# S5 mixer and gate placed between the blocks of the input projection, and prompt and decode cross attention interleaved, with cache loads issued earlier

## Chip, cores and metric

The kernel is written in Bass and runs on one core of one Trainium2 chip. The metric is the device time of one execution in microseconds (us). The kernel before takes 1489.02 us, the median of three runs (1488.8 to 1489.31).

## The reference

One layer of a hybrid decoder. A prompt of 512 tokens and 8 decode requests of 8 tokens each go through the same weights; the kernel treats them as T = 576 columns. All tensors are float32, D = 1024.

```
h = x + 1/2 * SwiGLU(rms_norm(x))                      # w_ffn1, F = 2816
u = rms_norm(h);  q,k,v,zg,r,us5 = split(u @ w_in)     # 256,256,512,16,512,512 columns
GLA (4 heads, dk 64, dv 128): log_a = log_sigmoid(zg @ w_gate + b)/16,
    S_t = diag(a_t) S_{t-1} + k_t^T v_t,  o_t = q_t S_t;  o = rms_norm(o) * silu(r)
S5 (32 groups x 16 channels, 64 complex states): x_t = A x_{t-1} + B u_t,
    y = Re(C x) + D u;  z = gelu(y);  out = z * sigmoid(z @ w_glu + b)
h = h + concat(GLA, S5) @ w_out
mk, mv = split(rms_norm(mem_prompt) @ w_ckv)           # 256 memory tokens, 4 heads of 256
h = h + CrossAttn(rms_norm(h) @ w_cq, keys, values) @ w_co
    # the prompt attends to mk, mv; each decode request to its own cached keys and values
h = h + 1/2 * SwiGLU(rms_norm(h));  y = rms_norm(h)    # w_ffn2
```

The new GLA and S5 states and mk, mv are outputs too. The cached keys and values of a request are 256 x 1024 numbers each, 1 MB; there are 8 of each.

## The kernel before

**Projections.** Every weight matrix is cut into blocks of 128 output columns, in the order of the list `groups` (first feed-forward, W_IN, W_IN+1, W_OUT mixed with KV, W_Q, W_O, second feed-forward). SP loads block n into one of four buffers `raw`; it waits until block n-4 has been converted. ACT's `conv(n)` copies it to a high half `wh` (L1102), DVE's `conv(n)` forms the low half `wl` (L1365), both two blocks ahead of PE. PE's `dense` does three products (high-high, high-low, low-high) in 8 k steps and two column halves of 288: 48 matmuls of L604 a block, into PSUM banks 0 to 3. DVE evicts a block when PE has finished it, and `ps_free` and `w_lo` let the block after next go. Most PE instructions that are not turns (transposes) go through one helper, L604.

**Input projection.** W_IN gives q, k, v, W_IN+1 gives r and the S5 input u; both write `PR`. Between the two, ACT issues eight DMAs that spread Kt into TT (L1180). Behind W_IN+1 PE does the 16-column gate rank (h, wzg).

**S5 and gate stage.** It starts when all projection blocks are done. PE turns u (L741), turns it again into u2 (L749), does the gate's products, the input products (Win x u2, stationary from Hs), the products with TT, then those with XS and CA, turns of states (L790 to L792), of v (L799), of the gelu result z (L811), and the GLU products. Between these DVE and ACT work: copies out of PSUM (L1525, L1529), ACT's crosswise copies (L1202), rotation by tables (L1540 to L1543), one scan over all chunks (L1546), rotation back (L1549 to L1553), the gate's log and its scans, gelu (L1216), copies of v (L1618) and z (L1621), then sigmoid (L1232), product (L1627), high copy (L1235), low half (L1637). POOL builds keep5 (L571) and scales q (L574). Level operations for GLA (L1579 to L1590) are put between the sigmoid steps. GLA's seven levels follow: PE's small products, and `take` on DVE (L1598).

**Cross attention.** When W_Q is done, the prompt's four row blocks of 128 go one after another: scores (8 products), maxima on DVE (L1749), exponentials on ACT (L1307), division on DVE (L1754), eight turns on PE (L1000), copy (L1761); the next block's scores are issued ahead. Then eight value products of 512 columns, twice each. Only then the eight decode requests: 16 turns of the keys (L1016) in two halves, copied by ACT (L1325) and DVE (L1787), with scores of 32 stationary columns a head; then decode softmax and values. SP loads the caches (L377) into four buffers `KB`, keys 0 and 1 when W_Q is done, keys 2 and 3 when the last prompt scores are, the rest as buffers come free.

Of the kernel before, what the change touches and what calls it, by code (L numbers as in the profile page):

```python
# [6 lines left out]
F32 = mybir.dt.float32  # L7
# [6 lines left out]
P = 128  # L14
# [37 lines left out]
def hymba_kernel(nc, A, O, consts):  # L52

    with ExitStack() as ctx:
# [90 lines left out]
        kem = view(AR, 4 * T, NB, 2, DK)  # L145
# [32 lines left out]
        u2 = view(Xs, 0, G, C5)  # L178
        SF = Xs[:, 2304:6400]
        UT = SF[0:C5, :].rearrange("p (g s q) -> p g s q", g=G, s=L5)  # L180
        zin = view(SF, 0, G, C5P)
        zz = view(SF, 2048, G, C5P)
        Y2 = SF[0:C5, :].rearrange("p (t j) -> p t j", t=L5)
        SG = Xs[:, 6400:8704]
        XS = view(SG, 0, G, C5)
        keep5 = view(SG, 0, G, C5P)
        wglu = view(Xs, 8704, 4, P)
        zin_tmp = SF[:, 2048:4096]
        zT = view(SG, 0, 4, T)
        sig = view(Xs, 0, T)  # L190
        sog = view(Xs, 576, T)
        s1o = view(MM, 8448, 3, P)

        Snew = view(AR, 12 * T, 2, NB, DV)
# [3 lines left out]
        mh = view(ARr, 8 * T, KD, M)  # L198
# [6 lines left out]
        KB = [view(Xs, 4096, 2, D), view(Xs, 6144, 2, D), view(MM, 0, 2, D), view(MM, 2048, 2, D)]  # L205
        KBT = view(MM, 8192, KD, M)
        pp = view(Xs, 0, H, M)
        att = view(Xs, 1024, 16)
        os = view(Xs, 1040, 2, M)

        qz = view(Xs, 2048, KD, NB, 4 * BT)
        PTz = view(MM, 4096, 2, H, NB, 4 * BT)
# [12 lines left out]
        def add(kind, src, nblk, K, row0, cols, **kw):  # L225
            n0 = sum(g["n"] for g in groups)
            groups.append(dict(kind=kind, src=src, n=nblk, K=K, row0=row0, cols=cols, n0=n0, **kw))
# [10 lines left out]
        add("proj", A["w_in"], 8, KD, 0, (0, P, 2 * P), f0=0, first=True)  # L238
        add("proj", A["w_in"], 8, KD, 0, (D + RANK, D + RANK + P, 2 * P), f0=8)
# [54 lines left out]
        def _(e):  # L294
# [31 lines left out]
            def load(n):  # L326

                g, i = blocks[n]
                K, (c0, c1, step) = g["K"], g["cols"]
                col = (i // 2) * step + (c0, c1)[i % 2]  # L330
# [18 lines left out]
            load(3)  # L349
            for n in range(4, groups[W_O]["n0"] + 4):  # L350
                load(n)
                if n % 2:
                    parameters((n - 3) // 2)
                if n == groups[W_OUT]["n0"] + 5:
                    e.wait_ge(S("zt_mm"), L5)
# [11 lines left out]
            for n in range(2 * NB):  # L367
                if n < 2:
# [231 lines left out]
        def _(e):  # L600
# [171 lines left out]
            for r in range(8):  # L772
                if r == 4:
                    e.wait_ge(S("d_ok"), 5)
# [1084 lines left out]
```

## Time and profile before

| | |
|---|---|
| median of three runs | 1489.02 us |
| profiled execution, its own time | 1489.69 us |
| its span in the profile | 1487.9 us |
| mean granted clock of PE | 0.956 |
| busy: PE, weight loads, DVE, ACT, POOL | 93%, 89%, 46%, 28%, 19% |
| bytes moved | 130.2 MB, 88 GB/s |

The time of an execution is a little longer than the span between its first and last recorded instruction. A granted clock of 1.0 is 2.4 GHz, 0.5 is 1.2 GHz; a value between is the mean of a stretch with both. A matrix product in float32 leaves two records a matmul, a turn one. Positions in the trace are us from the start of the span.

### The profile page before, as it was taken

What the parts mean: (1) busy time and instruction counts of PE and PEld (TensorE: products, weight loads), DVE (VectorE), ACT (ScalarE), POOL (GpSimd) and SP (SyncE); (2) the same over time, 40 slices, a digit from 0 to 9 for tenths busy, and PEclk for the clock granted to TensorE, in tenths of its full rate; (3) what the DMA queues carried; (4) which work ended last, traced back from release to release, by engine and by line L of the source; (5) the groups of instructions that cost most, each with busy time, mean ns of one, the idle gap of its engine ahead of it and who ended that gap; (6) DMA issues with size and microseconds to landing.
All of it is one profiled execution on the core that took longest, in us unless ns stands there. A gap on an engine that the chain in (4) does not pass through costs nothing.

```text
span 1487.9 us, 24142 instructions
## 1 busy us (share of the span) xinstructions
PE 1383.2 (93%) x10626; PEld 1324.0 (89%) x10626; DVE 689.2 (46%) x817; ACT 422.6 (28%) x550; POOL 287.1 (19%) x372
## 2 busy tenths in 40 slices
PE   5999999999999989866799996989999999999997
PEld 4999999999998988856789894559999999999997
DVE  5444258635444324786664534324443334433442
ACT  4322122212234111452443212213422122212233
POOL 3001799887022002000011000003100000000012
PEclk9999999999999999776899997989999999999998
DMA  6433222322222352010144342462223222232221
GB/s 167 98 90 85 86 72 85 86 86 72 75 82 57 85 102 74 1 33 6 57 130 140 97 148 81 142 226 86 73 84 86 86 86 78 79 86 85 78 65 65
DMA packets 227049, 130.20 MB, mean 88 GB/s; under 512 B 22192, under 2 KB 221296, under 8 KB 226928
## 3 DMA queue, kind: packets, MB, share of 16 engines
q1 hardware_dynamic: 219552, 123.22, 28.6%
q10 hardware_dynamic: 7392, 5.43, 1.7%
q8 instruction: 84, 1.38, 0.4%
q14 instruction: 21, 0.17, 0.0%
HBM read 121.67 MB, written 5.78 MB: 86 GB/s over the span
## 4 chain that ended last, share of the span: by engine, by line
PE 84%; DVE 10%; ACT 2%; issue 2%; DMA 1%; ACTq 1%; POOLq 0%; POOL 0%; DVEq 0%
PE PS L604 80%; DVE wl L1365 1%; PE PS L1016 1%; ACTq L1180 1%; DMA AR<-in_cache_mem_v 1%; DVE gua L1442 1%; ACT Xs L1307 1%; DVE AR L1598 0%; PE PS L1000 0%; DVE Xs L1754 0%; DMA gua<-in_g_mem 0%; DVE AR L1761 0%; DVE Xs L1749 0%; DVE Xs L1621 0%; DVE Xs L1546 0%
## 5 line engine op out<-in xcount | busy, mean ns | idle before, releaser
L1102 ACT ACTIVATE wh<-raw 128x1024 fp32r<-128x1024 f32 (+1 forms) x192 | 200.6, 1045 | 794.8 <-PE PS L604 794.8
L604 PE MATMUL PS<-xh,wh 128*128 128x288 f32 x1792 | 388.1, 298 | 16.4 <-DVE wl L1365 11.0
L604 PE MATMUL PS<-xh,wl 128*128 128x288 f32 x1792 | 385.7, 297 | 0.0
L604 PE MATMUL PS<-xl,wh 128*128 128x288 f32 x1792 | 385.3, 297 | 0.0
L604 PEld LDWEIGHTS PS<-xh,wh 128*128 128x128 f32 x1792 | 290.3, 190 | 18.8 <-DVE wl L1365 12.2
L604 PEld LDWEIGHTS PS<-xh,wl 128*128 128x128 f32 x1792 | 290.5, 190 | 0.0
L604 PEld LDWEIGHTS PS<-xl,wh 128*128 128x128 f32 x1792 | 290.4, 190 | 0.0
L1365 DVE TENSOR_TENSOR wl<-raw,wh 128x1024 fp32r<-128x1024 f32 (+1 forms) x192 | 259.1, 1349 | 56.6 <-ACT wh L1102 54.9
L407 POOL TENSOR_TENSOR acc<-acc,sq 128x576 f32<-128x576 f32 x40 | 68.0, 1700 | 772.8 <-issue 537.4
L604 PE MATMUL PS<-yh,wh 128*128 128x288 f32 x960 | 207.6, 298 | 1.0 <-DVE yl L1802 1.0
L604 PE MATMUL PS<-yl,wh 128*128 128x288 f32 x960 | 206.3, 297 | 0.0
L604 PE MATMUL PS<-yh,wl 128*128 128x288 f32 x960 | 206.0, 296 | 0.0
L604 PEld LDWEIGHTS PS<-yh,wh 128*128 128x128 f32 x960 | 155.3, 190 | 1.6 <-DVE yl L1802 1.4
L604 PEld LDWEIGHTS PS<-yl,wh 128*128 128x128 f32 x960 | 155.4, 189 | 0.0
L604 PEld LDWEIGHTS PS<-yh,wl 128*128 128x128 f32 x960 | 155.3, 189 | 0.0
L1417 DVE SCALAR_TENSOR_TENSOR h<-PS,h 128x576 f32<-128x576 f32 x56 | 42.4, 758 | 191.0 <-PE PS L604 191.0
L416 POOL TENSOR_TENSOR AR<-AR 128x32 f32<-128x32 f32 (+6 forms) x168 | 112.1, 667 | 13.6 <-POOL AR L529 0.4
L1439 DVE TENSOR_TENSOR gua<-PS,R 128x576 f32<-128x576 f32 x44 | 33.4, 758 | 156.2 <-PE PS L604 156.1
L1435 DVE TENSOR_TENSOR gua<-PS,R 128x576 f32<-128x576 f32 x44 | 33.3, 756 | 108.3 <-PE PS L604 108.3
L604 PE MATMUL PS<-AR 64*64 64x64 f32 (+5 forms) x640 | 63.8, 345 | 7.1 <-DVE AR L1598 3.7
L604 PEld LDWEIGHTS PS<-AR 64*64 64x64 f32 (+3 forms) x640 | 44.8, 175 | 24.9 <-issue 10.1
L1507 DVE TENSOR_TENSOR AR<-PS,R 128x576 f32<-128x576 f32 x24 | 18.2, 757 | 88.8 <-PE PS L604 75.4
(297 smaller groups left out, 1108.8 us busy)
## 6 DMA issues: line engine op xcount, KB each, us to landing
raw<-in_w_ffn_gu SPq DMA_DIRECT2D x88, 512.0 KB, 3.8
raw<-in_w_ffn_down SPq DMA_DIRECT2D x32, 512.0 KB, 4.0
raw<-in_w_in SPq DMA_DIRECT2D x16, 512.0 KB, 4.0
raw<-in_w_ckv SPq DMA_DIRECT2D x16, 512.0 KB, 3.9
raw<-in_w_ffn_down SPq DMA_DIRECT2D x16, 384.0 KB, 3.4
raw<-in_w_out SPq DMA_DIRECT2D x8, 512.0 KB, 4.4
raw<-in_w_cq SPq DMA_DIRECT2D x8, 512.0 KB, 4.2
raw<-in_w_co SPq DMA_DIRECT2D x8, 512.0 KB, 4.2
```

What stands on the lines that cost most here:

```text
L407: e.tensor_tensor(acc[:, 0:T], acc[:, 0:T], sq[:, k % 2, :], ALU.add).then_inc(acc_ready, 1)
L416: own(TTT(o, a, b, ALU.mult))
L604: return e.matmul(out, lhsT, rhs, start=start, stop=stop, **kw)
L1016: last = e.transpose(bank(0, P, at=f * M + j * P), KB[b % 4][:, j, f * P:(f + 1) * P], ident)
L1102: e.activation(wh[:, n % 2, 0:K * P], raw[:, n % 4, 0:K * P], ACT.Copy).then_inc(w_hi, 1)
L1180: e.dma_start(TT[P5 * s:P5 * s + P5, :, P5 * s:P], Kt[:, :, 0:P - P5 * s]).then_inc(S("tt_in"), 16)
L1307: e.activation(pp[0:w, hd, :], bank(4 * (1 - r % 2), H, M, rows=w)[:, hd, :], ACT.Exp, bias=att[0:w, 4 + hd:5 + hd], scale=CD ** -0.5, acc ...
L1365: TTT(wl[:, n % 2, 0:K * P], raw[:, n % 4, 0:K * P], wh[:, n % 2, 0:K * P].bitcast(F32), ALU.subtract).then_inc(w_lo, 1)
L1417: STT(two(hk), halves(2 * par), 0.5 if g["half"] else 1.0, two(hk), ALU.mult, ALU.add).then_inc(ps_free, 1)
L1435: TTT(two(gs[:]), halves(0), two(R[:]), ALU.mult).then_inc(g_scaled, 1)
L1439: TTT(two(us[:]), halves(2), two(R[:]), ALU.mult).then_inc(ps_free, 1)
L1507: TTT(two(chunk(PR, f)), halves(2 * par), two(R[:]), ALU.mult).then_inc(ps_free, 1)
```

## The change

It has two parts.

- The input projection is one run of 16 blocks in the order u, q, k, v, r. PE's S5 and gate work is cut into pieces, and `beside(b, i)` issues one behind k step i of block b: gate rank in block 4, turns of u in 5, of u2 in 6, input products in 7 and 8, gate products in 10, TT and XS products in 11 and 12, turns of z in 13, of v in 14, GLU in 15. DVE's and ACT's `beside(b)` do their share behind their work for block b. The small products use banks 4 to 7 only, and the S5 buffers have moved to Hs and AR. TT's DMAs are issued by SP, two behind each of four weight loads; copies of v are ACT's now, and every second copy of z.
- Cross attention is written as one hand-made order on PE, DVE and ACT: turns of a request's keys, decode scores of the request before, and every third step the scores, turns or values of a prompt row. Keys are copied by head instead of by half. Decode scores run with f outside and heads inside. Keys 0 to 3 are loaded during the W_Q blocks into Hs, 4 and 5 when W_Q is done; the values each have a place of their own as soon as it is free. Waits for `gla_out` come before W_Q on DVE, `kv_out` on ACT moves to W_O.

The core of the diff:

```diff
-        add("proj", A["w_in"], 8, KD, 0, (0, P, 2 * P), f0=0, first=True)
-        add("proj", A["w_in"], 8, KD, 0, (D + RANK, D + RANK + P, 2 * P), f0=8)
+        add("proj", A["w_in"], 8, KD, 0, [D + RANK + (4 + i) * P for i in range(4)] + [i * P for i in range(4)])
+        add("proj", A["w_in"], 8, KD, 0, [(4 + i) * P for i in range(4)] + [D + RANK + i * P for i in range(4)])
...
+                if n > groups[W_Q]["n0"] and (n - groups[W_Q]["n0"]) % 2 and n < groups[W_O]["n0"]:
+                    e.wait_ge(mm_done, M0 + MIX.rindex("W") + 3)
+                    load_cache((n - groups[W_Q]["n0"]) // 2)
...
+                s0 = 2 * (n - groups[W_IN]["n0"] - 5)
+                if 0 <= s0 < L5:
+                    e.wait_ge(S("tt_zero"), 1)
+                    e.wait_ge(S("ktd_ok"), 1)
+                    for s in (s0, s0 + 1):
+                        e.dma_start(TT[P5 * s:P5 * s + P5, :, P5 * s:P], Kt[:, :, 0:P - P5 * s]).then_inc(S("tt_in"), 16)
...
+            def beside(b, i):
+
+                if b == 4:
+                    gate_rank(i)
+                elif b == 5:
+                    turn_u(i)
+                elif b == 6 and i < 5:
+                    turn_u2(i)
+                elif b == 7 and i % 3 == 0:
+                    input_products(i // 3)
+                elif b == 8 and i in (1, 4):
+                    input_products(3 + i // 4)
+                elif b == 10 and i in (0, 2):
+                    gate_products(i // 2)
+                elif b in (11, 12) and i % 2:
+                    s5_outputs(4 * (b - 11) + i // 2)
+                elif b == 13:
+                    turn_z(i)
+                elif b == 14 and 2 <= i < 7:
+                    turn_v(i - 2)
+                elif b == 15 and i % 2:
+                    glu(i // 2)
+
+            n0 = groups[W_IN]["n0"]
+            for b in range(16):
+                dense(n0 + b, b % 2, KD, xh, xl, ready=(x_lo, 8) if b == 0 else None,
+                      inside=(lambda: rms(1), KD - 3) if b == 0 else None, each=lambda i: beside(b, i))
+            e.wait_ge(ps_free, n0 + 18)
+            e.wait_ge(S("sig_ok"), 4)
...
+            def decode_scores(b):
+                if b == 0:
+                    e.wait_ge(S("qz_ok"), 4)
+                e.wait_ge(S("kbt_a"), 2 * b + 2)
+                e.wait_ge(S("kbt_v"), 2 * b + 2)
+                for f in range(2):
+                    for hd in range(H):
+                        last = mm(PS[32 * hd:32 * hd + 32, 7, (b // 4) * M:(b // 4 + 1) * M], qz[:, 2 * hd + f, b, :],
+                                  KBT[b % 2][hd][:, f, :], start=(b % 4 == 0 and f == 0), stop=(b % 4 == 3 and f == 1),
+                                  skip_group_check=True)
...
+            turn_keys(0)
+            prompt_scores(0)
+            turn_keys(1)
+            decode_scores(0)
+            turn_keys(2)
+            decode_scores(1)
+            prompt_scores(1)
+            prompt_turn(0)
+            turn_keys(3)
+            decode_scores(2)
...
+            decode_scores(7)
+            prompt_turn(3)
+            decode_values(0)
+            for f in range(4):
+                prompt_values(f)
+            decode_turn(1)
+            for f in range(4, 6):
+                prompt_values(f)
+            decode_values(1)
+            decode_out_turn(0)
+            for f in range(6, 8):
+                prompt_values(f)
+            decode_out_turn(1)
...
-            for s in range(L5):
-                e.dma_start(TT[P5 * s:P5 * s + P5, :, P5 * s:P], Kt[:, :, 0:P - P5 * s]).then_inc(S("tt_in"), 16)
...
+            def beside(b):
...
+                elif b == 9:
+                    rotate_back(0)
+                    e.wait_ge(S("z_mm"), 1)
+                    for i in range(2):
+                        mark(TSC(two(zb[:, i, :]), halves(4 + 2 * i), bgate[:, i:i + 1], None, ALU.add), "z_sb")
```

## Rows read from the trace of the kernel before

**Rows 1.** The page, busy time and share of the span by engine.
```profile
PE 1383.2 (93%) x10626; PEld 1324.0 (89%) x10626; DVE 689.2 (46%) x817; ACT 422.6 (28%) x550; POOL 287.1 (19%) x372
```
**Rows 2.** Stretches: length, busy PE, PEld, DVE, ACT, POOL, then clock, DMA, GB/s.
```profile
592.20:667.55 75.35, 57.78 (x420) 51.40 (x419) 60.35 (x82) 34.49 (x56) 4.36 (x7) 0.77 0.07 19
602.00:620.00 18.00, 18.00 (x89) 18.00 (x90) 12.68 (x23) 8.66 (x14) 0.00 (x0) 0.53 0.00 1
620.00:624.00 4.00, 4.00 (x39) 4.00 (x38) 3.96 (x2) 1.69 (x2) 0.49 (x1) 1.00 0.00 0
...
888.20:995.00 106.80, 83.29 (x521) 50.49 (x521) 39.85 (x70) 23.57 (x55) 5.47 (x7) 0.86 0.48 168
```
**Rows 3.** Timeline of PE, S5 stage: start, length, line, shapes, count, idle before.
```profile
592.22 3.72 PE L741 MATMUL PS<-cst,AR 128*72 128x128 f32 x32
596.81 2.20 PE L749 MATMUL PS<-cst,Xs 72*128 72x72 f32 x32 [0.87 <-DVE Xs L1525]
...
601.91 13.62 PE L604 MATMUL PS<-Xs,Hs 128*128 128x72 f32 x64
...
628.63 8.85 PE L604 MATMUL PS<-AR,Xs 128*72 128x128 f32 x64 [4.19 <-DVE Xs L1553]
...
652.89 6.50 PE L604 MATMUL PS<-Xs 128*128 128x288 f32 x16 [0.83 <-DVE Xs L1621]
```
**Rows 4.** Timelines of ACT's queue and of PE between W_IN and W_IN+1.
```profile
526.71 13.47 ACTq L1180 DMA_DIRECT2D Hs<-AR  x8
...
544.28 0.85 PE L604 MATMUL PS<-xh,wh 128*128 128x288 f32 x2 [4.95 <-DVE wl L1365]
```
**Rows 5.** Chain that ended last, one prompt row's softmax: start, length, what.
```profile
908.34 1.24 DVE Xs L1749
...
909.80 1.94 ACT Xs L1307 x8
```
**Rows 6.** The same chain, decode keys and scores, then decode values.
```profile
946.75 1.02 PE PS L1016 x8
947.77 0.99 PE PS L604 x8
...
976.57 3.75 PE PS L604 x64
...
980.34 10.28 DMA AR<-in_cache_mem_v
```
**Rows 7.** The same chain, turns of mk and mv inside a W_Q block.
```profile
846.90 0.44 PE PS L971 x4
847.34 0.80 PE PS L604 x6
```
**Rows 8.** Timeline of DVE in the S5 stage.
```profile
618.96 4.42 DVE L1546 TENSOR_TENSOR_SCAN Xs<-Xs 128x2048 f32<-128x2048 f32 x1
...
655.99 0.76 DVE L1627 TENSOR_TENSOR Xs<-Xs 128x576 f32<-128x576 f32 x1 [1.76 <-ACT Xs L1232]
...
667.55 1.33 DVE L1598 COPY_PREDICATED AR<-cst,PS 128x512 f32<-128x512 int32 x2
```
**Rows 9.** Groups of 584 to 668, and line L1365 (duration ns min/median/max, 200 to 300).
```profile
L1365 DVE TENSOR_TENSOR wl<-raw,wh 128x1024 fp32r<-128x1024 f32 x1 | 4.1, 4061 | 0.4 <-ACT wh L1102 0.4
L574 POOL TENSOR_SCALAR AR<-AR 128x1152 f32<-128x1152 f32 x1 | 4.0, 3985 | 0.1
...
L1365 DVE TENSOR_TENSOR wl<-raw,wh x16: 1225/2182/3425, 200.6 to 297.2; 128x1024 fp32r<-128x1024 f32 x16
```
**Rows 10.** Timeline of PE in the cross attention.
```profile
898.22 1.10 PE L1000 MATMUL PS<-cst,Xs 128*128 128x128 f32 x8 [2.00 <-DVEq L1755]
...
906.88 3.62 PE L604 MATMUL PS<-AR 128*128 128x256 f32 x16
...
925.58 16.26 PE L604 MATMUL PS<-AR 128*128 128x512 f32 x32 [1.32 <-DVE AR L1761]
```
**Rows 11.** Stretch after that first gap, columns as in rows 2.
```profile
900.00:902.00 2.00, 2.00 (x6) 1.58 (x5) 1.93 (x3) 0.00 (x0) 0.00 (x0) 0.50 0.04 8
```

More of the change, by code:

```diff
@@ L1199, in _, with swap @@
                     e.wait_ge(S("d_ok"), r - 1)
-                d, dw = bank(4 + r % 4, n, C5), view(zin_tmp, 512 + 512 * (r % 2), n, C5P)
+                d, dw = bank(4 + r % 4, n, C5), dw_buf[r % 2][:, 0:n * C5P].rearrange("p (g c) -> p g c", g=n)
                 for a in (0, 64):
                     e.activation(dw[64 - a:128 - a], d[a:a + 64, :, 0:C5P], ACT.Copy).then_inc(S("dw_ok"), 1)
-            e.wait_ge(S("z_sb"), 2)
-            mark(e.activation(zt, zb, ACT.Abs), "act_own")
-            mark(e.activation(zt, zt, ACT.Exp, scale=-1.0), "act_own")
-            mark(e.activation(zt, zt, ACT.Ln, bias=one[:]), "ln_ok")
-            for half in range(2):
+            def swap(half):
                 gg = slice(16 * half, 16 * half + 16)
@@ L1210, in _, with gelu @@
                 e.activation(zin[0:64, gg, :], zz[64:128, gg, :], ACT.Copy).then_inc(S("swap_a"), 1)
-            e.wait_ge(S("s1_ok"), 1)
-            e.wait_ge(S("swap_a"), 2)
-            for r in range(8):
+            def gelu(r):
                 e.wait_ge(S("y_mm"), r + 1)
@@ L1237, in _ @@
+            n0 = groups[W_IN]["n0"]
+            for b in range(16):
+                if b == 0:
+                    rms(1)
+                conv(n0 + b + 2)
+                beside(b)
+            e.wait_ge(S("y_mm"), 8)
+            e.activation(EB, zb, ACT.Exp, scale=1.0 / TAU).then_inc(S("eb_ok"), 1)
             for j in range(NT):
@@ L1310, in softmax_decode @@
             def softmax_decode(c):
[L1311 to L1317 removed]
+                e.wait_ge(S("mx_ok"), ROWS["decode"][c])
+                e.activation(ppd[:, c, :], bank(7, M, at=c * M), ACT.Exp, bias=attd[:, 4 + c:5 + c],
+                             scale=CD ** -0.5, accum_out=attd[:, 8 + c:9 + c]).then_inc(S("exp_ok"), 1)
@@ L1319, in _ @@
                 e.activation(yh[:, f, 0:TP], bank(4 + f % 2, TP), ACT.Copy).then_inc(S("pv_hi"), 1)
[L1320 to L1327 removed]
+            e.wait_ge(gla_out, 64)
@@ L1328, in _, with decode_high @@
+            keep_keys(0)
+            softmax(0)
+            keep_keys(1)
+            keep_keys(2)
+            softmax(1)
+            keep_keys(3)
+            keep_keys(4)
+            softmax(2)
+            softmax_decode(0)
+            keep_keys(5)
+            keep_keys(6)
+            softmax(3)
+            keep_keys(7)
             softmax_decode(1)
-            for c in range(2):
+            for f in range(6):
+                values_high(f)
+            def decode_high(c):
                 e.wait_ge(S("ost_mm"), c + 1)
```

715 lines of the change are left out of this document (409 added, 306 removed).

## Prediction

> **What bounds the kernel now.** The page's busy times come first: PE works in 93% of the span, so only three things can be won: time in which PE stands idle, time in which it runs at half its clock, and PE work itself [rows 1]. Next the stretches: two stages are neither projections nor feed-forward, and PE is poorly used in both. From the end of the input projection's rank-16 products (592.2) to the first predicated copy of the GLA levels (667.55) lie 75.4 us, with PE busy for 57.8 and a mean granted clock of 0.77. The cross attention, from the last query block to the first w_co matmul (888.2 to 995.0), takes 106.8 us, PE busy 83.3, clock 0.86 [rows 2]. Then the timelines say why. In the first stage PE, DVE and ACT hand the S5 work to one another. PE was busy all through 602 to 620, but at 0.53 of its clock; at the full clock, 620 to 624, it issues 39 records in 4 us [rows 2, 3]. Before that stage there is one more stop, at 544.28: PE had waited 4.95 us for a low weight half, because ACT was issuing eight DMAs (TT from Kt) for 13.47 us ahead of its conversions [rows 4]. In the second stage the softmax of each of the four prompt rows is a round trip PE, DVE, ACT, DVE, PE [rows 5], and near its end PE waits for the value caches: one DMA stands in the chain with 10.28 us [rows 6].
>
> **S5 and gate beside the projection.** The same PE instructions are issued, but between the k steps of sixteen dense blocks. That this costs no more than the instructions themselves is seen where the kernel does it already: four transposes take 0.44 us, the six matmuls behind them 0.80, and no gap is left [rows 7]. 6 in 0.80 makes 6.4 us for a block of 48; this is in both kernels and drops out, as do the rank-16 products.
> What is inserted, at the full clock: 32 turns of u 3.7; 32 turns for u2 2.2; 32 turns of z in the same 72x72 shape 2.2; 20 turns of v at u's 0.117 each 2.3 [rows 3]. Input products: 64 records took 13.62 at half clock, so 6.8. TT and XS: 128 records at 4.00/39 are 13.1 [rows 2, 3]. Gate and GLU: 16 records took 6.50 at half clock, so 24 at 0.2 are 4.9 [rows 3]. Three state turns 0.4. Sum 36 us. The upper bound is the pace of before, some 55 us, which they would cost only if PE fell to half clock; between dense matmuls it has no reason to.
> DVE and ACT have to keep up. DVE was busy 60 us in the old stage [rows 2]; with sixteen evictions (0.76, the price of 576 columns) and low halves (1.23) that is 92 us in about 16 x 6.4 + 8 + 36 = 146 [rows 8, 9]. So DVE is no bound over the whole, but single blocks can be late. I followed block by block (E8 is the end of dense block 8): the rotation of chunk 4 ends at E8 + 4.1, the scan takes 4.42 [rows 8], so DVE comes 2.2 us late to block 9's eviction. A low half has about 4 us of slack, so dense work does not stop there. But rotate_back(0) and the gate's bias come behind, and S5 output 0 in block 11 waits for z_sb: 1 to 4 us. ACT puts Abs, Exp, Ln ahead of the next conversion, rotate_back(1) comes behind that, and gelu behind s1_ok: up to 1 us in block 12. The GLU of block 15 waits for sigmoids that stand behind five ACT operations and a table load: 1.3. First turns in blocks 6, 7 and 13: 0.1 to 0.5 each. That is about 5 together.
> POOL adds to it. It now scales q (3.98 us) and builds keep5 beside the u2 copies and the first rotations. Where these two ran before, DVE's low half took 4.06 us against 1.23 at best [rows 9]. So I add 2 us of stall for the chain pushed later, with 0 and 5 as bounds. The Trainium skill, "SBUF — State Buffer", Who interferes with whom, says that VectorE and GpSimd share a port pair which one of them holds for a whole instruction while the other is blocked. The rows agree, 4.06 against 1.23; by that rule every DVE operation with two SBUF inputs that meets one of POOL's waits out its rest, by these rows up to 2.8 us a meeting, and two meetings in a row would make the 2 us a 5.
> **The tail.** After block 15 DVE finishes the sigmoid chain (sigmoid, product, copy and subtraction at some 0.75 each, about one and three quarters rounds late: 5.1), then evicts (0.8), converts (1.25), forms KE over 1152 columns (1.4), and does four pairs of level operations at 0.7 each that before were hidden in the wait for sigmoids (5.7): 14.3 us to the first predicated copy [rows 8]. This part stays exposed, and GLA after it is untouched.
> Before: 75.4, plus 4.95 for the stop at 539 and 1.5 for a restart at half clock [rows 2, 4]. After: 36 + 7 + 14.3 = 57.3. **Gain 24.5 us**, bounds 5 (all that is inserted at half clock) and 33 (no stall, tail 2 shorter).
> The TT DMAs go to SP's queue, two behind each of four weight loads: 13.47 us of issue in all [rows 4], over four blocks of 6.4. Behind them stand only weight loads issued about three blocks ahead of use, so nothing is late; if that cover were gone, the stop of 5 us would come back. UT shares memory with Kt, so DVE and ACT wait for tt_in in block 5; by then the last has been issued for about a block. The eight small DMAs of wglu stay on ACT, ahead of need.
>
> **Cross attention.** PE work after, at full clock: four prompt scores at 3.62 are 14.5; four turns of probabilities at 1.02 are 4.1; eight key turns of 16 transposes at 2 x 1.02 are 16.3; the prompt's values 13.8: 16 products of 512 columns, twice the 0.45 of 256 would be 14.5, and 16.26 is what they took with half clock in front, from which I take off its first 2.5 [rows 6, 10]. Decode scores: before, four products on two column groups took 0.99, so 15.8 in all; the new order runs f outside and heads inside, so four column groups follow one another as in the decode values, where 32 products took 3.75, or 0.94 for eight. I take 8 x 0.94 = 7.5 as that row has the same pattern; the other bound is 15.8 [rows 6]. Decode values 7.5, small turns 2.3. Sum 66 us.
> Idle: in each of four rounds DVE takes the maxima (1.24 and 0.18), ACT the exponentials (1.94) [rows 5], and ACT's key copies stand behind them, so the third or fourth quarter of a key turn waits about 2.5 us: 9 with the last DVE steps. Clock: the gap of 2.0 us before 898.22 was enough to leave 900 to 902 at 0.50 [rows 10, 11]; by that row the 2.5 us gaps can each cost 1.7 more; I add 3 of 7. End of the stage: 66 + 9 + 3 = 78 against 106.8 and 1.5 for the slow restart of w_co. **Gain 30.3 us**, bounds 18 and 38.
> The caches: K0 to K3 go out in the query blocks, behind weight loads with slack. The other 12 have 78 us; before, they moved in 46 (945 to 991), so the 10.28 us leave the chain [rows 6]. V7 waits on the third decode values product (about 54 us in) and is used at 65: 11 us against a landing of 10.3 at worst; 0 to 3. The w_co weights from the fifth on stand behind V7 on SP, but are used 20 us later. The earlier waits for gla_out find DMAs issued 80 us before, and POOL's memset of PTz ends about a microsecond ahead of need: nothing.
>
> **Sum.** 1489.69 (the profiled execution; span 1487.9) - 24.5 - 30.3 = 1434.9; the median of the runs is 0.67 lower, so 1434.2.
>
> **Rivals.** (a) The round trips cost less: 2 us of stalls in S5, none for the clock, 2 fewer in attention: 1434 - 5 - 3 - 2 = 1424. For: each wait rests on an order that I guessed. (b) Decode scores stay at 0.99 per four (+8.3) and each attention gap halves the clock (+4): 1446. For: the rows show both; against: the row of the values [rows 6, 11]. The Trainium skill, "TensorE: Matmul & The Clock Gate", HAM oscillation, tells that repeated waits bring the slow clock back every time; the window at 900 agrees. (c) The S5 chain is a block late somewhere, through POOL or ACT's order: 6.4 and some 7 more idle, 1448. (d) Slower than before: PE works in order, so an S5 piece that waits for DVE now stops dense matmuls too. With eleven blocks that carry pieces this is slower than before from 5.2 us of waiting per block (57 over 11). The largest wait for DVE in front of these pieces was 4.19 us, once [rows 3], and DVE has 92 us of work in 146: unlikely; 1500. (e) The change does not do what it says: the pieces wait until the projection is over, or cache loads hold up weights: 1480 to 1489.
>
> **How the numbers follow.** Forecast 1434 (1427 to 1442) 0.50; (a) 0.17; (b) 0.13; (c) 0.14; (e) 0.03, of which 0.02 within 0.2% (3 us, about what a measurement can tell); (d) 0.03. The range 1416 to 1456 leaves out (d), (e) and the outer parts of (a) and (c), some 0.15. Faster 0.95, same 0.02, slower 0.03.
>
> **What would show it.** No gap in front of the second half of the input projection; its blocks 5 to 15 at clock 1.0, 36 us longer together than 6.4 each; a gap of 1 to 4 us in block 11; about 14 us from the last GLU product to the first predicated copy; an attention of 78 us, with eight decode score products in 0.94 and no cache DMA in the chain. A block longer than its sum by over 5 us, half clock in the projection, or scores at 2 us for eight would make it wrong.

## The result and the profile after

| kernel | median, us | lowest to highest | ratio to before, 95% interval |
|---|---|---|---|
| before | 1488.91 | 1486.32 to 1489.31 | 1 |
| after | 1438.53 | 1437.9 to 1438.6 | 0.9664 [0.9648, 0.9681] |

The change takes 50.4 us off, 3.4%; 1434.2 was forecast. The profiled execution of after has a span of 1436.7 us, 51.2 less than the 1487.9 of before, and a mean granted clock of 0.973 (0.956 before).

The page of after, first the busy line that answers to [rows 1], then the chain that ended last by engine:

```profile
PE 1352.5 (94%) x10626; PEld 1303.9 (91%) x10626; DVE 682.3 (47%) x816; ACT 428.1 (30%) x567; POOL 287.3 (20%) x372
...
PE 86%; DVE 9%; ACT 3%; issue 2%; DMA 0%; ACTq 0%; POOLq 0%; POOL 0%; DVEq 0%
```

The number of PE records is the same, 10626. PE is busy 31 us less because it does the same work at a higher clock (and with more products side by side), and stands idle 20 us less. The stretches of after that answer to [rows 2], same columns (length, busy time of PE, PEld, DVE, ACT, POOL, clock, DMA share, GB/s): first the whole input projection with the S5 pieces in it up to the first predicated copy, a piece inside it, the tail behind the last GLU product, then the attention from the last query block to the first w_co product, and two pieces inside it.

```profile
472.92:643.03 170.11, 158.40 (x1231) 145.24 (x1231) 89.92 (x110) 62.99 (x88) 11.58 (x9) 0.97 0.28 64
602.00:620.00 18.00, 18.00 (x151) 17.45 (x150) 10.47 (x16) 9.01 (x12) 0.26 (x1) 1.00 0.21 59
628.47:643.03 14.56, 5.32 (x88) 4.02 (x88) 12.26 (x16) 9.28 (x14) 0.00 (x0) 0.59 0.42 108
865.25:945.08 79.83, 67.44 (x522) 45.51 (x520) 41.28 (x78) 23.93 (x63) 4.31 (x6) 0.96 0.49 172
860.00:900.00 40.00, 33.10 (x261) 27.54 (x259) 20.76 (x34) 13.08 (x39) 1.99 (x4) 1.00 0.51 184
900.00:920.00 20.00, 16.33 (x127) 11.98 (x127) 11.39 (x24) 5.02 (x14) 2.32 (x2) 0.83 0.57 211
```

The same stretch of before, from the first product of the input projection to the first predicated copy, is this one. It holds nearly the same records (1223 against 1231) in 23.4 us more:

```profile
474.05:667.55 193.50, 170.98 (x1223) 158.90 (x1223) 98.40 (x120) 53.98 (x75) 11.98 (x9) 0.90 0.25 57
```

The attention went from 106.80 us [rows 2] to 79.83. So the 51.2 us are: 1.1 before the input projection starts (474.05 to 472.92), 23.4 in it and the S5 stage, 27.0 in the attention, 1.3 behind it, less 1.6 between the first predicated copy and the end of W_Q (220.6 us before, 222.2 after). That last 1.6 is no effect of the change that these traces can show: the same kernel took 218.6 us there in another execution, and kernels whose edits lie elsewhere 221.2 to 222.1.

Where PE now stands idle. In the projection and S5 stage, its timeline shows one stop of any size among the dense blocks, the first S5 output in block 11, which waits for the gate's bias; the pieces behind it come every 3.34 us, two k steps of 0.80 and 1.74 of their own. The idle time is in brackets with what ended it.

```profile
574.14 1.06 PE L633 MATMUL PS<-Hs,AR 128*72 128x128 f32 x8 [1.97 <-DVE gua L1723]
...
577.50 1.04 PE L633 MATMUL PS<-Hs,AR 128*72 128x128 f32 x8
...
624.68 1.24 PE L633 MATMUL PS<-AR,Hs 128*128 128x288 f32 x4 [0.37 <-ACT sq L1359]
627.34 1.13 PE L633 MATMUL PS<-AR,Hs 128*128 128x288 f32 x4
635.31 2.42 PE L633 MATMUL PS<-AR 64*64 64x64 f32 x72 [6.84 <-DVE AR L1807]
```

The stop of 4.95 us [rows 4] is gone. In the attention PE waits for ACT's copies of turned keys (L1456) and for the decode softmax:

```profile
875.19 0.66 PE L1095 MATMUL PS<-cst,Hs 128*128 128x128 f32 x4 [2.67 <-ACT Xs L1456]
...
887.46 0.66 PE L1095 MATMUL PS<-cst,Hs 128*128 128x128 f32 x4 [1.79 <-ACT Xs L1456]
...
900.26 0.66 PE L1095 MATMUL PS<-cst,Xs 128*128 128x128 f32 x4 [2.32 <-ACT Xs L1456]
...
913.93 0.41 PE L1114 MATMUL PS<-cst,Xs 128*128 128x128 f32 x2 [3.00 <-DVE AR L1947]
...
945.08 0.54 PE L633 MATMUL PS<-yh,wh 128*128 128x288 f32 x2 [1.72 <-DVE yl L1985]
```

### The profile page after: what moved, and what is told of

Its sections match the earlier page's. It is cut to its first block, busy times and chain, and to the rows that moved or that the text cites. A ratio compares the mean times of both kernels' runs of the same rounds, so it can differ in the third digit from the quotient of the medians.

```text
span 1436.7 us, 24185 instructions
## 1 busy us (share of the span) xinstructions
PE 1352.5 (94%) x10626; PEld 1303.9 (91%) x10626; DVE 682.3 (47%) x816; ACT 428.1 (30%) x567; POOL 287.3 (20%) x372
## 3 DMA queue, kind: packets, MB, share of 16 engines
q1 hardware_dynamic: 223280, 124.40, 30.3%
## 4 chain that ended last, share of the span: by engine, by line
PE 86%; DVE 9%; ACT 3%; issue 2%; DMA 0%; ACTq 0%; POOLq 0%; POOL 0%; DVEq 0%
PE PS L633 83%; DVE wl L1524 1%; PE PS L1095 1%; DVE gua L1601 1%; DVE AR L1791 0%; ACT wh L1209 0%; DMA gua<-in_g_mem 0%; ACT Xs L1442 0%; DVE Xs L1935 0%; PE PS L724 0%; DVE Hs L1718 0%; DVE Xs L1830 0%; DVE xl L1641 0%; DVE xl L1555 0%; DVE h L1645 0%
## 5 line engine op out<-in xcount | busy, mean ns | idle before, releaser
L633 PE MATMUL PS<-AR 64*64 64x64 f32 (+6 forms) x720 | 73.3, 339 | 13.8 <-DVE AR L1791 6.8
L633 PEld LDWEIGHTS PS<-AR 64*64 64x64 f32 (+4 forms) x720 | 52.7, 178 | 28.0 <-issue 13.4
L633 PE MATMUL PS<-ARr,wh 128*128 128x256 f32 x256 | 46.1, 282 | 0.8 <-DVE wl L1524 0.8
```

What stands on the lines that cost most here:

```text
L633: return e.matmul(out, lhsT, rhs, start=start, stop=stop, **kw)
```

## The experiments

Theory: the gain is PE's time, won in two independent stages; what is left lies in the tail behind the GLU and in the order in which ACT copies keys. Rivals: the stages depend on each other; the low price of the decode scores is a matter of their order; the early loads bring nothing; the slack of the S5 chain is large, or small. Eleven further kernels were run, and the kernel after once more. The kernel before ran beside each group; its median was between 1488.6 and 1490.2. The second time, after itself had a median of 1437.39 us with single executions from 1433.57 to 1441.0. By medians alone, then, only five kernels lie clear of after: the two single parts, the early outputs, and the new copy order alone and in the pair. For the others the cause is read from the waits and lengths in their traces.

### Each part alone

The S5 part with the attention of before, and the attention part with the S5 stage of before. In words, since the edits are the two halves of the diff; the one line added, in the first, keeps a wait where the new placement needs it:

```diff
+            e.wait_ge(gla_out, 64)      # DVE, now ahead of its W_Q group
```

> The S5 part of the change with the attention of the kernel before. My theory: the two parts don't touch each other, so this kernel keeps the gain read between the start of the input projection and the first predicated copy (193.50 to 170.20 us, 23.3), and loses about 1.4 us of it again in the W_Q stage: 1489 - 22 to 24 = 1465 to 1467 us. Its attention stage, from the last W_Q product to the first projection of the cross stage, is again about 107 us. Rival: the stages are coupled by the clock, and the gap of 14.7 us between the last gate product and the first predicated copy costs more in this kernel than in the whole change; then the time is 1470 or more.

Measured: 1463.85 us, ratio 0.9828 [0.9814, 0.9843], so 25.3 us gained, a little more than the 22 to 24 expected.

> The attention part of the change with the S5 stage of the kernel before. My theory: its gain is its own, 106.8 to about 80 us for the stage and so 1489 - 26 to 28 = 1461 to 1463 us; the two gains add up to the 50.4 of the whole. Rival: the early cache loads are hidden only because the S5 stage of the whole change left the DMA queues earlier, or they take from the weight transfers of W_Q; then less than 24 us are gained here and the sum of the two single kernels falls short of the whole by more than 2 us.

Measured: 1463.3 us, 0.9820 [0.9805, 0.9835], so 25.8 gained. The two make 51.1; the whole change gains 50.4. The stages don't depend on each other, and the early cache loads work without the new S5 stage. The attention part came out a little under its range of 26 to 28. In the attention of the first kernel PE still waits for the value caches, as in [rows 6], here at each of four groups of products, the longest time 2.40 us:

```profile
961.28 1.96 PE L612 MATMUL PS<-Xs,AR 128*32 128x256 f32 x16 [2.40 <-DMA Xs<-in_cache_mem_v]
```

### The order of the decode scores

```diff
-                for f in range(2):
-                    for hd in range(H):
+                for hd in range(H):
+                    for f in range(2):
```

> The changed kernel with one edit: the decode score products run over the halves of the contraction inside and the heads outside, as in the kernel before, so that two products that follow each other go to the same column group. My theory: the eight products of a batch took 0.94 to 1.07 us in the changed kernel because the four heads' products overlap, and in the kernel before a batch of four took 0.99 (eight records in 1.98 with both halves); this edit brings the second figure back for 8 batches: +0.9 each, +7 to 8 us, 1445 to 1447. Rival one: the overlap is between any products of different column groups however they are ordered, and the order costs half: +3 to 4, 1442. Rival two: the order does nothing, because the stage is held by the copies of the turned keys: within 1 us of 1438.5.

Measured: 1439.07 us, 0.9657 [0.9641, 0.9673]: nothing, as in rival two, but not for its reason. PE's timeline, first of after, then of this kernel; each x2 line is one product of two records, and the last line of each is the turn behind the eight.

```profile
888.05 0.41 PE L633 MATMUL PS<-Hs,AR 128*32 128x256 f32 x2
...
888.29 0.39 PE L633 MATMUL PS<-Hs,AR 128*32 128x256 f32 x2
...
889.05 2.06 PE L1095 MATMUL PS<-cst,Xs 128*128 128x128 f32 x16
```

```profile
888.86 0.42 PE L633 MATMUL PS<-Hs,AR 128*32 128x256 f32 x2
...
889.10 0.39 PE L633 MATMUL PS<-Hs,AR 128*32 128x256 f32 x2
...
889.88 2.07 PE L1095 MATMUL PS<-cst,Xs 128*128 128x128 f32 x16
```

Eight products take 1.00 us from the first to the turn in the one and 1.02 in the other. The prediction's reason, that heads inside lets column groups follow one another, falls. The size, 0.94, was right. What remains as a difference from before is how many column groups are at work between two instructions that take all columns: four here, two before. The next run tests that.

```diff
-            decode_scores(b)            # b = 0, 2, 4
-            turn_keys(b + 2)
+            decode_scores(b, (0, 1))
+            turn_keys(b + 2, (0, 1))
+            decode_scores(b, (2, 3))
+            turn_keys(b + 2, (2, 3))
```

> The changed kernel with the decode score products of batches 0, 2 and 4 parted: heads 0 and 1, then half of the key turns of batch b+2, then heads 2 and 3 and the other half. The order of the eight products did nothing (they took 1.07 us in either order), and in the kernel before four products of two heads, between key turns on all columns, took 0.99. My theory: what sets their time is how many column groups are at work between two products that take all columns: the records of one group follow each other (0.4 us each product), those of four groups overlap. Each half then takes 0.95 to 1.05 us and each parted batch 0.9 to 1.0 us more: +2.7 to +3 us in all, 1441 to 1441.5. Rival: the price belongs to the waits on the copies in the kernel before, not to the column groups: each half takes about 0.5 and the time stays within 0.5 us.

Measured: 1442.12 us, 0.9671 [0.965, 0.9693], some 3.6 us over after. PE's timeline:

```profile
889.26 0.66 PE L1095 MATMUL PS<-cst,Hs 128*128 128x128 f32 x4 [1.79 <-ACT Xs L1460]
889.85 1.06 PE L633 MATMUL PS<-Hs,AR 128*32 128x256 f32 x8
890.84 1.10 PE L1095 MATMUL PS<-cst,Xs 128*128 128x128 f32 x8
891.86 1.06 PE L633 MATMUL PS<-AR 128*32 128x256 f32 x8
892.85 1.42 PE L1095 MATMUL PS<-cst,Xs 128*128 128x128 f32 x8
894.21 1.07 PE L633 MATMUL PS<-Xs,AR 128*32 128x256 f32 x16
```

Each half takes 0.99 (889.85 to 890.84, 891.86 to 892.85): the price of before for four products, 0.99 [rows 6]. The unparted batch behind them (894.21, x16) takes 1.00 again. The parted batch costs 0.98 more, and its second eight turns 0.34 more than the first (1.36 from start to next start against 1.02), which the theory didn't have: 1.3 a batch. The same 0.34 stands at all three parted batches; its cause is open. By medians 3.6 us were measured for 2.7 to 3 expected. The theory holds for the scores: four products on two column groups cost what eight on four do, in either order. That it isn't a fixed price of each entry is seen in [rows 6]: there 64 records on four groups, 16 a group, took 3.75, or 0.23 for each record of a group; here four a group take 1.00, or 0.25. An estimate from these rows: with all eight batches in halves, as before, the scores would cost 8 us more.

The Trainium skill, "TensorEngine Tiling (Array Packing)", Key Properties, states that tiles operate independently and can execute in parallel. The rows agree and add that this held here whether the next product in order went to the same group or to another.

### The small DMAs on ACT

```diff
-                    for s in (s0, s0 + 1):            # SP, beside four weight loads
-                        e.dma_start(TT[...], Kt[...]).then_inc(S("tt_in"), 16)
+                if b == 1:                            # ACT, behind block 1
+                    for s in range(L5):
+                        e.dma_start(TT[...], Kt[...]).then_inc(S("tt_in"), 16)
```

> The changed kernel with the transfers that build the mixer's block matrix issued from ScalarE's stream, behind its second block, and not from SyncE's beside the weights. My theory of the 4.95 us wait on the second weight half in the kernel before: ScalarE's share of these issues had delayed what the block waits for. If so, ScalarE comes late with its copies by the time of the issues (8 of about 0.6 to 1.3 us, 5 to 8 us in all), TensorE waits for a copy once, and 3 to 6 us of the gain go: 1441 to 1445. Rival: ScalarE has that slack in the early blocks of the projection, and nothing changes: 1438 to 1439.5.

Measured: 1444.04 us, 0.9695 [0.9677, 0.9713]: 5.5 over after, the upper end. ACT's queue and, below it, PE:

```profile
486.35 14.09 ACTq L1307 DMA_DIRECT2D Hs<-AR  x8
...
502.91 0.55 PE L627 MATMUL PS<-xh,wh 128*128 128x288 f32 x2 [3.94 <-DVE wl L1523]
```

The eight issues take 14.09 us, as the 13.47 of [rows 4], and not the 5 to 8 that the expectation wrote down against its own row. The stop in front of a block is back, 3.94 us. On SP in after the four pairs take 1.33, 1.26, 2.78 and 2.46 us, 7.8 in all and not the 13.47 that the prediction carried over, and PE has no wait there.

### Late cache loads

```diff
-                if n > groups[W_Q]["n0"] and (n - groups[W_Q]["n0"]) % 2 and n < groups[W_O]["n0"]:
-                    e.wait_ge(mm_done, M0 + MIX.rindex("W") + 3)
-                    load_cache((n - groups[W_Q]["n0"]) // 2)
...
-            for n in range(4, 2 * NB):
+            for n in range(2 * NB):
```

> The changed kernel with all cache transfers issued behind the last W_Q block, so none is there when the attention starts. In the changed kernel a transfer lands 7.2 us (median) after its issue, and the key turns of the first batch start at once. My theory: the first key turn comes some 5 to 7 us late, because a first transfer needs that long; behind it the 16 transfers keep ahead of TensorE (each about 3.7 us of a queue share, against 9 us of TensorE a batch), so the loss is that first wait plus a clock that starts low: +5 to +9 us, 1443.5 to 1447.5. Rival one: the transfers in a bunch share the DMA engines and land later one by one, so that each batch waits: +15 or more, as in the kernel before. Rival two: TensorE's scores of the prompt stand ahead of the keys in its order only from the second place; the wait is longer than any cover: nothing is hidden, +7 to +9 with the full latency. An unchanged time would say that the early loads bring nothing.

Measured: 1443.44 us, 0.9687 [0.9665, 0.9708], 4.9 over after. PE's timeline where the attention starts, and the stretch of the whole attention in this kernel:

```profile
871.39 3.68 PE L1092 MATMUL PS<-cst,Hs 128*128 128x128 f32 x16 [5.07 <-DMA Hs<-in_cache_mem_k]
...
866.17:953.10 86.93, 70.78 (x522) 47.72 (x521) 41.05 (x78) 24.15 (x63) 4.34 (x6) 0.90 0.56 206
```

One wait of 5.07 us, then 16 turns at 3.68 in place of 2.06 because the clock is halved behind it, and no further wait for a cache. The attention is 7.1 us longer than in after, which is the first wait and the clock (0.90 for 0.96). Rival one, every batch waiting, is out; theory and rival two gave nearly the same time (the measured one is just under both), and what tells them apart is the wait, within the theory's 5 to 7. The whole profiled execution is 8.0 us longer than after's. Of that 1.6 lie in the S5 stage, where nothing was edited: PE's wait in block 11 is the same, 1.96, but here the clock was lower behind it (0.91 over 560 to 580, 1.00 in after).

### How much slack the S5 chain has

```diff
+                elif b == 10 and i >= 4:
+                    s5_outputs(i - 4)
-                elif b in (11, 12) and i % 2:
-                    s5_outputs(4 * (b - 11) + i // 2)
+                elif b == 11 and i % 2:
+                    s5_outputs(4 + i // 2)
```

> The changed kernel with the eight output pieces of the state mixer put half a block to a block earlier on TensorE: the first four in the second half of the projection's block 10, the other four in block 11, none in block 12. It measures how much slack the mixer's chain has: in the changed kernel the first of these pieces waits 2.0 us for VectorE's copy of the gate input at 572.4. My theory (the mechanism of my slower case): TensorE takes its instructions in order, reaches the first piece at about 568, and stands until about 572 with all of the block's products behind it; VectorE's eviction doesn't come earlier for it. The wait is 4 to 6 us in place of 2, and the later pieces wait for ScalarE's gate steps of the block before: +2 to +5 us, 1440.5 to 1443.5. Rival: VectorE is ready by then because its own order depends on TensorE's block 9 only, and nothing changes: 1438 to 1439.

Measured: 1451.0 us, 0.9739 [0.9724, 0.9754]: 12.5 over after, far outside the expected 2 to 5. PE's first stop, DVE's line behind it, PE's second stop, and two stretches:

```profile
573.55 1.95 PE L633 MATMUL PS<-Hs,AR 128*72 128x128 f32 x8 [5.96 <-DVE gua L1725]
...
584.31 0.76 DVE L1809 TENSOR_TENSOR AR<-PS,R 128x576 f32<-128x576 f32 x1 [10.87 <-PE PS L633]
...
592.18 1.98 PE L633 MATMUL PS<-Hs,AR 128*72 128x128 f32 x8 [4.65 <-ACT Hs L1306]
...
570.00:590.00 20.00, 13.99 (x94) 13.77 (x94) 8.55 (x10) 7.21 (x6) 0.00 (x0) 0.82 0.12 36
590.00:600.00 10.00, 7.82 (x49) 7.82 (x50) 1.35 (x2) 2.28 (x8) 1.09 (x2) 0.67 0.01 2
```

The first wait is as expected, 5.96 us, 4.0 more than after's. But a second of 4.65 follows, for ACT's gelu (L1306), and the first one feeds it. PE stood inside block 10, so that block ended late; DVE had to wait 10.87 us for it before its eviction (584.31). Behind the eviction and the low half stands the second half of the rotation back, which ends at 591.4; gelu starts at 591.48 when it is there, and PE's fifth output piece waits for gelu. PE waits for DVE, which waits for PE: the expectation had counted only the first half of that circle. And behind each wait the clock is halved for a while: 13.99 x 0.18 + 7.82 x 0.33 = 5.1 us. Waits of 8.6 more and 5.1 for the clock make 13.7; the stage is 183.73 us long against 170.11. So the chain does not have the slack of half a block to a block that this edit takes, and the mechanism of rival (d) is real: this one placement costs a quarter of the whole change's gain.

### GpSimd beside VectorE

```diff
+            for _ in range(3):
+                own(TTT(keep5, ..., ALU.mult))
             mark(TTT(keep5, ..., ALU.mult), "keep_ok")
```

> The changed kernel with GpSimd's product that builds the keep mask (3.63 us at 533.59) done four times, so that GpSimd works some 11 us longer beside VectorE's eviction, low half and first two rotations (535.3 to 545). In the changed kernel its one meeting with VectorE's low half stretched that from 1.23 to 1.89 us and TensorE did not notice. My theory: each VectorE operation with two SBUF inputs that meets a GpSimd operation waits for it to end; operations that read PSUM on one side don't. Low half and the rotation's second and third operations (0.62 each, four of them up to 545) are stretched, two to four meetings of 1 to 3 us; VectorE is 5 to 8 us late in block 7, the low half of the block after next has only some 4 us of slack, so TensorE stops for 1 to 4 us, and the clock may halve behind it: +1 to +5 us, 1439 to 1443. Rival: TensorE's slack swallows it all (as it did the one meeting), within 1 us of 1438. Second rival: both engines share and GpSimd's operations are the ones stretched; then VectorE's durations stay 0.62.

Measured: 1441.3 us, 0.9671 [0.9649, 0.9694], 2.8 over after. POOL's timeline (three of the four products in one line), then DVE's beside it, then PE's stop in block 11:

```profile
533.62 12.15 POOL L601 TENSOR_TENSOR AR<-AR,cst 128x2048 f32<-128x2048 f32 x3 [1.74 <-DVE AR L1709]
545.85 3.88 POOL L603 TENSOR_TENSOR AR<-AR,cst 128x2048 f32<-128x2048 f32 x1
...
538.81 0.62 DVE L1681 TENSOR_TENSOR Hs<-PS,AR 128x448 f32<-128x448 f32 x1 [0.48 <-ACT Hs L1297]
539.47 2.83 DVE L1682 TENSOR_TENSOR Hs<-Hs,AR 128x448 f32<-128x448 f32 x1
542.33 3.93 DVE L1683 TENSOR_TENSOR Hs<-Hs 128x448 f32<-128x448 f32 x1
...
576.08 1.06 PE L636 MATMUL PS<-Hs,AR 128*72 128x128 f32 x8 [3.88 <-DVE gua L1726]
576.98 1.72 PE L636 MATMUL PS<-AR 128*72 128x128 f32 x8
```

DVE's operations with both inputs in SBUF (L1682, L1683) took 2.83, 3.93 and (at 547.25) 2.98 us in place of 0.62; the ones with PSUM on one side (L1681) kept their 0.62 in the same time. These three cost DVE 7.9 us. PE noticed none of it before block 11, where its wait grew from 1.97 to 3.88, and 1.6 more went because the clock dropped behind it (the next piece came 4.94 us later, not 3.36): 3.5 us of stage, 646.55 against 643.03. Only the 1.9 of waiting is surely POOL's: with late caches the same 1.6 came behind an unchanged wait. Of the rivals, the first is out by the wait in the trace, not by the median, and the second by DVE's durations. The Trainium skill, "SBUF — State Buffer", Who interferes with whom, states a lock: whichever of a DVE operation with two SBUF inputs and a GpSimd one starts first holds it for the whole instruction. The trace agrees, down to which operations are spared, and POOL's own three took 12.15 us where three times the 3.63 of after would be 10.9.

### Two orders improved

Run together with the changed kernel once more, five rounds each. First, the four level operations put into DVE's waits of the gate steps; second, ACT's first key copy of each odd batch ahead of the exponentials, and the decode row block's turn behind the scores of batch 6 (with a wait that the shared PSUM bank needs); third, both.

```diff
                         mark(TTT(sog, zT[:, f, :], sig, ALU.mult), "so_ok")
+                        (level_factors, level_rel)[f % 2](f // 2 + 2 * (f % 2))
                         e.wait_ge(S("mix_hi"), 1 + f)
...
-            level_factors(0)
-            level_rel(2)
-            level_factors(1)
-            level_rel(3)
```

```diff
             keep_keys(0)
-            softmax(0)
-            keep_keys(1)
+            keep_keys(1, (0,))
+            softmax(0)
+            keep_keys(1, (2,))
...
-            decode_turn(0)
             turn_keys(7)
             decode_scores(6)
+            decode_turn(0)
```

> The changed kernel once more, beside the three that follow, so that effects of less than one per cent are compared on one chip: 1438.5 us, within 1 us.

Measured: 1437.39 us (1433.57 to 1441.0), 0.9649 [0.9627, 0.9671]. Its profiled execution was the shortest of the four, with a span of 1431.8 us, 4.9 less than the first one of the same kernel.

> The changed kernel with the four level operations that stand behind the last copy to the key-end tile (0.67 to 1.3 us each on VectorE, about 5.4 us between the last gate step and the first predicated copy) put between the four gate steps, where VectorE waits 0.8 us for ScalarE in each. My theory: the tail's chain runs alternately through ScalarE and VectorE; 0.8 us of each operation is hidden in these waits and the tail of 14.7 us becomes 12 to 13: -2 to -3 us, 1435.5 to 1436.5. Rival one: ScalarE's own step isn't what VectorE waits for at that time, each operation delays the next gate step by its whole length, and nothing is gained: 1438 to 1439. Rival two: the first predicated copy is released by TensorE's level products that wait for the last evictions anyway, and TensorE's time behind moves the gain away: 1437.5 to 1438.5.

Measured: 1432.68 us, 0.9617 [0.9602, 0.9632], 4.7 under the run of after beside it; the intervals still touch. The trace has a surer number. DVE's timeline, first of after, then of this kernel:

```profile
633.70 0.76 DVE L1751 TENSOR_TENSOR yl<-sq,yh 128x576 fp32r<-128x576 f32 x1 [0.82 <-ACT yh L1362]
...
643.03 1.32 DVE L1791 COPY_PREDICATED AR<-cst,PS 128x512 f32<-128x512 int32 x2
...
646.60 1.33 DVE L1791 COPY_PREDICATED AR<-cst,PS 128x512 f32<-128x512 int32 x2 [2.06 <-PE PS L633]
```

```profile
635.52 0.75 DVE L1753 TENSOR_TENSOR yl<-sq,yh 128x576 fp32r<-128x576 f32 x1
...
639.38 1.33 DVE L1793 COPY_PREDICATED AR<-cst,PS 128x512 f32<-128x512 int32 x2
...
644.38 1.35 DVE L1793 COPY_PREDICATED AR<-cst,PS 128x512 f32<-128x512 int32 x2 [3.48 <-PE PS L633]
```

The last gate step is 1.8 us later, but 5.4 us of operations are gone from behind it: the first predicated copy is 3.65 us earlier, from the same start of the projection (472.92 in both). Not all of that is kept. PE's first level products wait for DVE's eviction behind the gate steps, so they start 1.8 us later than in after (637.12 against 635.31), and DVE, sooner ready for the next level, waits for PE 3.48 us in place of 2.06: the second pair of copies is 2.22 us earlier. So the edit is worth 2.2 us behind the first level, within the forecast 2 to 3, and the 4.7 by medians is more than its trace shows. Rival one is out. Rival two holds in part: 1.4 of the 3.65 moves into a wait for PE. (In the kernel with both edits that second copy comes 170.45 us behind the start of the projection, against 173.68 in after: 3.2, with PE at a higher clock just before it.)

> The changed kernel's attention with ScalarE's order changed: the first copy of the turned keys of each odd batch ahead of the four exponentials and not behind them; the decode row block's turn stands behind the scores of batch 6. In the changed kernel TensorE waits for that copy 2.67, 1.79 and 2.32 us, and 3.00 us for the decode row block, and TensorE's clock is halved from 900.8 to 918. My theory: the three waits of 6.8 us are nearly gone because the copy needs 0.7 us, the exponentials come 0.7 us later each, which the products behind hide; the clock is not lowered: -5 to -8 us, 1430 to 1433. Rival: the exponentials become the late ones (their chain over VectorE and ScalarE ends in the next turn), TensorE waits for the probabilities in place of the keys, and the gain is under 2 us: 1436.5 to 1438.5.

Measured: 1428.55 us, 0.9592 [0.9578, 0.9606], 8.8 under after beside it. PE's timeline, its stops in the attention:

```profile
872.76 1.53 PE L1095 MATMUL PS<-cst,Hs 128*128 128x128 f32 x12 [0.61 <-ACT Xs L1458]
...
893.91 0.41 PE L633 MATMUL PS<-Hs,AR 128*32 128x256 f32 x2 [1.71 <-ACT Xs L1449]
...
909.06 1.97 PE L1073 MATMUL PS<-cst,Xs 128*128 128x128 f32 x8 [1.68 <-DVEq L1949]
```

With 0.38 at the start, 0.60 at 906.31 and 1.72 at the end, PE is idle 6.7 us in this stage against 12.3 in after, and the stage takes 72.8 us against 79.8: 5.6 by the waits, the rest by the clock (0.98 for 0.96). So the stage gives 7.0 against the first trace of after, and 6.1 against the one taken beside it (78.9), inside the 5 to 8 expected; the rival is out. The medians' 8.8 is more than that, and the spans of the two executions taken side by side differ by only 4.5: the 6.1, and 2.3 of a projection that starts earlier (470.60, not 472.86), less 3.8 in the stages between and behind, where nothing was edited either. One of the new stops, 1.71, is the wait that was added for the bank.

> The two edits before this one together. My theory: they lie in different stages and add up: -7 to -11 us, 1428 to 1431. Rival: only one of them holds, and the time is that one's.

Measured: 1426.16 us, 0.9571 [0.9555, 0.9588]. The two add up in the trace: 166.5 us to the first predicated copy (638.47 less 472.00) for 170.1, and 72.7 in the attention. By medians it is 11.2 under after, at the far end of the 7 to 11 expected, and 63.5 under before (1489.68 beside it), the best of these kernels.

## Why the prediction was right

The forecast, 1434.2, was 4.3 under the measured 1438.5, inside the likeliest case's own range. By its own steps:

**S5 and gate beside the projection.** Forecast gain 24.5, measured 23.4 by the trace and 25.3 by the kernel with this part alone. The dense blocks ran at a clock of 1.00, the stop before the second half of the projection was gone, and the gap in block 11 was 1.97, between the 1 and 4 named. The terms inside were less good. Stalls were put at 5 and 2 for POOL and are 2.3 in all (1.97 and 0.37). POOL's share is zero here: q's scaling met copies out of PSUM and a low half that had begun before it, and the mask met one low half, 1.89 for 1.23. The run with the mask built four times shows the mechanism was real and its size off. The inserted work was put at 36 us and is about 41: what is left of 170.1 after 111.7 for everything else (before's 118.15 up to 592.20 less 4.95 and 1.5), 2.3 and 14.6 is 41.5. Most of the excess is in the small products: an output piece of 16 records takes 1.74 where 4.00/39 each would be 1.64, and a gate piece of four records 1.34 (562.23 to 565.17 is 2.94, less two k steps of 0.80) where 0.2 a record gave 0.8; the four GLU pieces, priced alike, take some 1.1 each. The two misses nearly cancel, which is luck: 4.7 us too much for stalls, 5.5 too little for the inserted work.

**The tail.** 14.3 forecast, 14.6 measured. Nothing on it was hidden, as said. The run with the level operations moved shows that 3.65 of it could be, of which 2.2 remain behind the next level.

**Attention.** Forecast 78 us, measured 79.8: PE work 64.8 for 66 (67.4 busy less 2.7 for the clock), idle 12.3 for 9, clock 2.7 for 3 (the eight scores at 900.85 took 1.86 in place of 1.00, the key turns of 902.71 and 914.17 2.69 and 3.32 in place of 2.06). The idle term was under-sized: the three waits for key copies are 2.67, 1.79 and 2.32, near the 2.5 forecast for each, but the decode softmax costs 3.0 alone, and three times 2.5 left only 1.5 of the 9 for all "the last DVE steps", of which the one before w_co takes 1.72. The restart of w_co is nearly at full pace (0.54 for the first two records, 0.43 settled). Gain with it 28.3 for 30.3.

**The decode scores.** The number was right (1.00 for 0.94) and the reason wrong: neither loop order matters; the number of column groups does. The row of the decode values pointed to the right price because it too used four.

**The caches.** No cache load in the chain, as forecast. Their early issue alone is worth 4.9 us by medians and 7.1 in the trace of the attention.

**Sum.** Of the 54.8 forecast, 1.1 is missing in the S5 stage, 2.0 in the attention, 1.6 between them, and 1.1 was gained ahead of it all: 51.2 by the spans.

**The rivals.** (a) came only for the stalls of the S5 stage (2.3); the attention has more idle time than forecast, and its clock cost nearly what was put. (b) has not come: scores at full concurrency, and half clock only behind two of the four gaps (900.26 and 913.93). (c): nowhere was the chain a block late; its longest wait was 1.97. (e): the pieces stand between the dense products, and PE shows no wait for weights in the W_Q blocks, where the early caches load. (d) did not occur, but the kernel with the outputs half a block to a block earlier shows that its mechanism begins closer than the prediction thought: it reckoned with 5.2 us a block over eleven blocks, while two waits were enough for 12.5 us. An estimate from this: four such places would cost the whole gain.

## What to carry to other kernels

Work of a serial chain can be put between the k steps of a long run of matmuls at nearly its own length (some 41 us here for 36 reckoned), if each piece is placed behind the time at which its input is ready; placed too early, it costs its wait, the next wait that this one causes, and the clock behind both, so placement is to be read from the timeline, not from sums of busy time. When PE waits for a copy that stands behind another engine's longer work, put the one copy that is due first ahead. With 32-column products keep four column groups at work between instructions that take all columns; their order doesn't matter.

## What the runs showed of the hardware

- A wait of the same length does not always lower PE's clock. The key turns behind a wait of 2.67 us took 0.66 in after (875.19), full speed, and 1.12 behind the same wait of 2.67 in the kernel with halves apart (its line is below). Even one kernel differs from itself: between two executions of after, whose waits in block 11 and for the key copies are the same to 0.01 us, the stage from the first predicated copy to the attention took 222.2 and 218.6 us, at a clock of 0.90 and 0.92. A difference of 1 to 4 us is therefore to be read from waits, not from medians.

```profile
874.30 1.12 PE L1095 MATMUL PS<-cst,Hs 128*128 128x128 f32 x4 [2.67 <-ACT Xs L1460]
```

  The prediction cited the Trainium skill, "TensorE: Matmul & The Clock Gate", HAM oscillation, for waits that bring the slow clock back every time. The page tells it of a kernel with longer waits, for DMA, in every round. The rows here agree in part: it came back behind some of these waits (once behind one of 1.96 us) and not behind others. What decides was not settled.
- Four fp32 products of 32 columns by 256 on two column groups took 0.99 us, eight on four 1.00, and the order of the eight changed nothing.
- Eight small DMAs issued in a row took ACT 13.47 and 14.09 us, while pairs of them took SP 1.26 to 2.78 us, 7.8 for all eight. Whether the engine or the pairing makes the difference was not tested.
